# The merge gates beside a triangular solve: eight wide pieces against seven narrow Strassen pieces

## What is computed

```python
rq, rk, rv, rg, gqkv, gz, ga, gb, mg_ret, mg_gdn = jnp.split(u @ w_in, SPLIT_IDX, axis=-1)
...
a_mat = jnp.einsum("bhnid,bhnjd->bhnij", kb, kc) * jnp.where(strict, decay_incl, 0.0)
lhs = jnp.eye(CHUNK) + a_mat
u = lax.linalg.triangular_solve(lhs, vc * bc, left_side=True, lower=True, unit_diagonal=True)
...
merged = jax.nn.sigmoid(mg_ret) * y_ret + jax.nn.sigmoid(mg_gdn) * y_gdn
return h + merged @ w_out
```

## Time and profile before

| what | value |
|---|---|
| median of three runs | 2882.27 us |
| the profiled execution, its own time | 2882.01 us |
| its span, first to last instruction | 2880.2 us |
| TensorE busy | 2747.2 us (95%) |
| DVE, ACT, POOL busy | 1401.9, 483.1, 164.8 us |
| chain that ended last | TensorE 83%, issue 10%, DVE 4% |
| mean granted TensorE clock | 0.973 |

### The profile page before, as it was taken

How to read it: one execution, slowest core, us unless ns; L and a number is a source line. 1 busy time by engine, 2 the same in 40 slices (tenths; PEclk the granted TensorE clock), 3 DMA queues, 4 the chain that set the end, 5 groups by cost and what they waited for, 6 DMA issues and landing times.

```text
span 2880.2 us, 41833 instructions
## 1 busy us (share of the span) xinstructions
PE 2747.2 (95%) x18538; PEld 2415.2 (84%) x18538; DVE 1401.9 (49%) x1876; ACT 483.1 (17%) x775; POOL 164.8 (6%) x155
## 2 busy tenths in 40 slices
PE   8999899999999989999999999899889989997998
PEld 5778788999687878899998877686789988876998
DVE  5573223895657232533331000156559766776454
ACT  1261110101136111110000000023121022112110
POOL 0002210000000321000000000000000001010000
PEclk9999999999999999999999999999789989998999
DMA  7341214885434212345445888735158634441442
GB/s 264 127 158 67 74 59 165 324 317 185 146 132 161 74 59 74 106 161 175 158 166 169 290 286 288 239 117 176 57 200 337 263 119 162 139 151 62 161 161 89
DMA packets 211924, 476.40 MB, mean 165 GB/s; under 512 B 7584, under 2 KB 36896, under 8 KB 211488
## 3 DMA queue, kind: packets, MB, share of 16 engines
q1 hardware_dynamic: 211168, 472.26, 47.0%
q10 hardware_dynamic: 576, 1.46, 0.1%
HBM read 472.64 MB, written 1.05 MB: 164 GB/s over the span
## 4 chain that ended last, share of the span: by engine, by line
PE 83%; issue 10%; DVE 4%; ACT 1%; DMA 1%; POOL 1%; SPq 0%; POOLq 0%; DVEq 0%; ACTq 0%
PE ps L462 17%; PE ps L1720 17%; PE ps L530 11%; PE ps L522 8%; PE ps L2229 7%; PE ps L1961 4%; PE ps L1915 4%; PE ps L2258 3%; PE ps L1168 1%; PE ps L1179 1%; PE ps L1175 1%; PE ps L2268 1%; PE ps L737 0%; PE ps L1041 0%; PE ps L2201 0%
## 5 line engine op out<-in xcount | busy, mean ns | idle before, releaser
L462 PE MATMUL ps<-uT,ring 128*128 128x256 f32 x1280 | 292.7, 384 | 18.6 <-DMA ring<-in_w_in 9.4
L462 PEld LDWEIGHTS ps<-uT,ring 128*128 128x128 f32 x1280 | 242.5, 193 | 51.3 <-issue 9.3
L2229 PEld LDWEIGHTS ps<-work,ring 128*128 128x128 f32 x1760 | 198.6, 192 | 5.1 <-issue 4.8
L2229 PE MATMUL ps<-work,ring 128*128 128x128 f32 (+4 forms) x1760 | 198.4, 275 | 0.0
L1720 PE MATMUL ps<-uT,ring 128*128 128x128 f32 x1584 | 192.0, 281 | 3.2 <-ACT uT L895 2.5
L1720 PEld LDWEIGHTS ps<-uT,ring 128*128 128x128 f32 x1584 | 188.1, 198 | 5.5 <-issue 5.2
L462 PE MATMUL ps<-xn,ring 128*128 128x256 f32 x768 | 174.2, 385 | 9.6 <-issue 6.9
L1720 PE MATMUL ps<-xn,work 128*128 128x128 f32 x1584 | 179.8, 275 | 0.0
L1720 PEld LDWEIGHTS ps<-xn,work 128*128 128x128 f32 x1584 | 178.3, 192 | 0.0
L462 PEld LDWEIGHTS ps<-xn,ring 128*128 128x128 f32 x768 | 146.7, 194 | 30.9 <-issue 11.3
L530 PEld LDWEIGHTS ps<-uT,ring 128*128 128x128 f32 x1152 | 135.4, 197 | 5.9 <-issue 5.8
(11 more groups left out here) (458 smaller groups left out, 4496.7 us busy)
## 6 DMA issues: line engine op xcount, KB each, us to landing
ring<-in_w_in SPq DMA_DIRECT2D x72, 1024.0 KB, 5.1
work<-in_ada_w SPq DMA_DIRECT2D x48, 1024.0 KB, 10.8
ring<-in_exp_w_down SPq DMA_DIRECT2D x40, 1024.0 KB, 5.1
ring<-in_attn_w_in SPq DMA_DIRECT2D x36, 1024.0 KB, 5.1
ring<-in_exp_w_gate SPq DMA_DIRECT2D x32, 1024.0 KB, 5.6
ring<-in_exp_w_up SPq DMA_DIRECT2D x32, 1024.0 KB, 6.4
ring<-in_ffn_w_in SPq DMA_DIRECT2D x32, 1024.0 KB, 7.4
ring<-in_ffn_w_out SPq DMA_DIRECT2D x22, 1024.0 KB, 8.4
```

What stands on the lines that cost most here:

```text
L462: mm = pe.matmul(acc[:, m * T:(m + 1) * T], w[:, k, m * P:(m + 1) * P], src[:, half * 4 + k, :], start=(half == 0 and k == 0 and m % 2 == ...
L2229: mm = pe.matmul(acc[:, m * c:(m + 1) * c], w[:, k, m * P:(m + 1) * P], picked[:, half * 4 + k, OFFS[i]:OFFS[i] + c], start=(half == 0 and ...
```

## The change

The four gate units of a layer are computed by Strassen's scheme on a half layer each: the unit's 1024 x 512 weights as 2 x 2 blocks of 512 x 256, the input as 2 x 2 blocks of 512 rows by 128 tokens. A unit then takes seven phases of eight products (128 x 128 weights, 128 tokens) in place of eight pieces of four. A half has 22 steps in place of 24. New on DVE: four sums of token blocks per layer (128 x 512), four weight sums per unit (128 x 1024, in place in the ring), four adds of output blocks per unit (128 x 256). New on ACT: four snaps per unit (128 x 256). The sigmoid works in place in SBUF after the last add. Both slabs of a unit are freed at P7. One PSUM bank holds two products' blocks, so P2 waits for the snap of P1, and P5 for that of P4.

```diff
-        BESIDE = (("mgret", 0), ("brret", 0), ("mgret", 1), ("brret", 1), ("mggdn", 0), ("mggdn", 1))
+        gate_tq = [area(4 + 0.5 * i, 512).rearrange("p (k t) -> p k t", t=P) for i in range(4)]
+        GATE_PHASES = ("P1", "P4", "P2", "P5", "P6", "P3", "P7")
+        def gate_phase_pe(pe, l, name, j, what):
...
+            if what == "P1":
+                slab_wait(pe, gate_slab[unit])
+                w, x_, to, start = A["A11"], B11, acc["a"], True
+            elif what == "P4":
+                slab_wait(pe, gate_slab[unit] + 1)
+                pe.wait_ge(gate_tq_ready, l + 1)
+                w, x_, to, start = A["A22"], T4, acc["d"], True
+            elif what == "P2":
+                pe.wait_ge(q_snap, 4 * Q + 1)
+                w, x_, to, start = A["A12"], B21, acc["b"], False
+            elif what == "P5":
+                pe.wait_ge(q_sum, 4 * Q + 1)
+                pe.wait_ge(q_snap, 4 * Q + 2)
+                w, x_, to, start = A["A22"], T1, acc["c"], False
+            elif what == "P6":
+                pe.wait_ge(q_sum, 4 * Q + 3)
+                pe.wait_ge(q_out, 4 * Q + 1)
+                w, x_, to, start = A["A11"], T2, acc["a"], False
+            elif what == "P3":
+                pe.wait_ge(q_sum, 4 * Q + 4)
+                pe.wait_ge(q_snap, 4 * Q + 3)
+                w, x_, to, start = A["A12"], B22, acc["c"], False
+            else:
+                pe.wait_ge(q_snap, 4 * Q + 4)
+                w, x_, to, start = A["A21"], T3, acc["a"], False
+            for m in range(2):
+                for k in range(4):
+                    mm = pe.matmul(to[:, m * P:(m + 1) * P], w[:, k, m * P:(m + 1) * P], x_[:, k, :],
+                                   start=(start and m == 0 and k == 0), stop=True, skip_group_check=True)
...
+            if half == 0:
+                return iter(gate("mgret", 0) + branch(0) + gate("mgret", 1))
+            return iter(branch(1) + gate("mggdn", 0) + gate("mggdn", 1))
...
-                for i in range(2):
-                    beside_pe(pe, l, 24 * half + 2 * (n - h0) + i)
-            for i in range(8, 12):
-                beside_pe(pe, l, 24 * half + i)
+                for i in range(2 if n + 1 < h0 + HALF else 1):
+                    next(beside)(pe)
+            for i in range(3):
+                next(beside)(pe)
...
+            act.wait_ge(q_out, 4 * quad_no[unit] + 4)
+            gate = sg[2 * (br == "gdn") + j]
+            act.activation(gate, gate, ACT.Sigmoid).then_inc(tick(sig_out), 1)
...
+                if half == 0 and n == 0:
+                    (B11, B12), (B21, B22) = token_blocks(uT)
+                    T1, T2, T3, T4 = gate_tq
+                    dstep(dve, dve.tensor_tensor(T1, B12, B11, ALU.subtract))
+                    dstep(dve, dve.tensor_tensor(T2, B22, T1, ALU.subtract))
+                    dve.tensor_tensor(T4, T2, B21, ALU.subtract)
+                    dve.tensor_tensor(T3, B22, B12, ALU.subtract).then_inc(tick(gate_tq_ready), 1)
...
+                if half == 0 and n < 3:
+                    gate_sums_dve(dve, early, *((0, 1), (2,), (3,))[n])
+                if half == 0 and n == 1:
+                    gate_add_dve(dve, early, early_sg, "11")
+            if half == 0:
+                gate_add_dve(dve, early, early_sg, "12", "21", "22")
...
+            if half == 1:
+                gate_sums_dve(dve, early, 0, 1, 2)
...
+                if lev == 3:
+                    if half == 0:
+                        merge_dve(dve, l, "ret", 0)
+                    else:
+                        gate_add_dve(dve, early, early_sg, "21", "22")
...
-                if half == 0 and lev == 2:
-                    merge_dve(dve, l, "ret", 0)
+                if half == 1 and lev == 1:
+                    gate_add_dve(dve, early, early_sg, "11")
+                    gate_sums_dve(dve, early, 3)
+                if half == 1 and lev == 2:
+                    gate_add_dve(dve, early, early_sg, "12")
+                if lev == 4:
+                    gate_sums_dve(dve, late, 0, 1, 2)
+                    if half == 0:
+                        dve.wait_ge(merged_out, 4 * l + 1)
+                    gate_add_dve(dve, late, late_sg, "11")
+                if lev == 5:
+                    gate_sums_dve(dve, late, 3)
+                if lev == 6:
+                    gate_add_dve(dve, late, late_sg, "12", "21", "22")
```

More of the change, by code:

```diff
@@ new lines, in gate_wait, with gate_snap_act @@
+        def gate_wait(eng, unit, what):
+            if what == "P7":
+                eng.wait_ge(slab_used, gate_slab[unit] + 2)
+            else:
+                eng.wait_ge(q_phase, Q_PHASES * quad_no[unit] + GATE_PHASES.index(what) + 1)
+        def gate_snap_act(act, unit, *which):
+            acc = gate_sums(unit)
+            where = {"P1": "a", "P4": "d", "P5": "c", "P6": "a"}
+            for what in which:
+                if what == "P1":
+                    act.wait_ge(q_out, 4 * quad_no[unit])
+                gate_wait(act, unit, what)
+                act.activation(gate_snap[what], acc[where[what]], ACT.Copy).then_inc(tick(q_snap), 1)
@@ new lines, in gate_sums_dve @@
+        def gate_sums_dve(dve, unit, *parts):
+            Q, A = quad_no[unit], gate_weights(unit)
+            for part in parts:
+                if part == 0:
+                    gate_wait(dve, unit, "P4")
+                    out_, a, b, op = "A22", "A21", "A22", ALU.add
+                elif part == 1:
+                    dve.wait_ge(q_sum, 4 * Q + 1)
+                    out_, a, b, op = "A21", "A11", "A21", ALU.subtract
+                elif part == 2:
+                    gate_wait(dve, unit, "P1")
+                    dve.wait_ge(q_sum, 4 * Q + 2)
+                    out_, a, b, op = "A11", "A22", "A11", ALU.subtract
+                else:
+                    gate_wait(dve, unit, "P2")
+                    dve.wait_ge(q_sum, 4 * Q + 3)
+                    out_, a, b, op = "A12", "A12", "A11", ALU.subtract
+                dve.tensor_tensor(A[out_], A[a], A[b], op).then_inc(tick(q_sum), 1)
@@ new lines, in gate_add_dve @@
+        def gate_add_dve(dve, unit, dst, *which):
+            Q, acc = quad_no[unit], gate_sums(unit)
+            f = lambda x: x.rearrange("p (m t) -> p m t", t=P)
+            d4 = dst.rearrange("p (m t) -> p m t", t=T)
+            for what in which:
+                i, t = int(what[0]) - 1, int(what[1]) - 1
+                out_ = d4[:, 2 * i:2 * i + 2, t * P:(t + 1) * P]
+                if what == "11":
+                    gate_wait(dve, unit, "P2")
+                    dve.wait_ge(q_snap, 4 * Q + 1)
+                    i_ = dve.tensor_tensor(out_, f(gate_snap["P1"]), f(acc["b"]), ALU.add)
+                elif what == "12":
+                    gate_wait(dve, unit, "P3")
+                    dve.wait_ge(q_snap, 4 * Q + 4)
+                    i_ = dve.tensor_tensor(out_, f(gate_snap["P6"]), f(acc["c"]), ALU.add)
+                elif what == "21":
+                    gate_wait(dve, unit, "P7")
+                    i_ = dve.tensor_tensor(out_, f(acc["a"]), f(gate_snap["P4"]), ALU.subtract)
+                else:
+                    i_ = dve.tensor_tensor(out_, f(gate_snap["P5"]), f(acc["a"]), ALU.add)
+                i_.then_inc(tick(q_out), 1)
+            if "22" in which:
+                free(unit)
@@ L1107, in beside_pe, with beside_steps, branch_pe @@
+        def beside_steps(l, half):
+            gate = lambda name, j: [lambda pe, what=what: gate_phase_pe(pe, l, name, j, what) for what in GATE_PHASES]
+            branch = lambda j: [lambda pe, i=i: branch_pe(pe, l, j, i) for i in range(8)]
+            if half == 0:
+                return iter(gate("mgret", 0) + branch(0) + gate("mgret", 1))
+            return iter(branch(1) + gate("mggdn", 0) + gate("mggdn", 1))
+        def branch_pe(pe, l, j, i):
+            name = "brret"
             part, m = i // 4 % 2, i % 4
@@ L1146, in solve_pe @@
             h0 = half * HALF
+            beside = beside_steps(l, half)
             spread(h0)
@@ L1169, in solve_pe @@
                 mm.then_inc(tick(psum_full), 1)
-                beside_pe(pe, l, 24 * half + 10 + 2 * lev)
+                next(beside)(pe)
                 pe.wait_ge(m_out, 6 * s + lev)
@@ L1180, in solve_pe @@
                 mm.then_inc(tick(psum_full), 1)
-                beside_pe(pe, l, 24 * half + 11 + 2 * lev)
+                next(beside)(pe)
             pe.wait_ge(x_out, 13 * s + 13)
@@ L1545, in decay @@
                 free(unit)
+            early = f"mgret{l}0" if half == 0 else f"mggdn{l}0"
+            late = f"mgret{l}1" if half == 0 else f"mggdn{l}1"
+            early_sg, late_sg = (sg[2 * half + j] for j in range(2))
             decay(h0)
```

58 lines of the change are left out of this document (45 added, 13 removed).

## The result

| | kernel before | with the change |
|---|---|---|
| median of six runs each, same chip | 2879.85 us (2877.52 to 2883.3) | 2891.47 us (2889.2 to 2894.72) |
| profiled execution, its own time | 2882.01 | 2893.02 |
| its span | 2880.2 | 2891.2 |
| TensorE, DVE, ACT, POOL busy | 2747.2, 1401.9, 483.1, 164.8 | 2750.7, 1458.9, 495.6, 173.4 |
| mean granted clock | 0.973 | 0.967 |

The ratio is 1.004, with an interval of 1.003 to 1.005: slower by 11.6 us where 2.1 was forecast, and above the range. 56 narrow phases took the place of 64 wide pieces, by the prediction's count 10.8 us less TensorE work at full clock, and yet TensorE is busy 3.5 us longer.

The account below looks back on a forecast made before the run. TensorE was taken to bound the solve, its chain having no gap. Fewer pieces, less added waits, restarts and tail delays, gave +2.1 us on 2882.01, so 2884.1 us; range 2876 to 2890, bounds 2877.8 to 2888.9.

Parts of the forecast that it names:

- The pieces and narrow phases: Gate units: eight wide pieces take 13.84 us, seven narrow phases 12.5; 10.8 less for eight units if nothing waits.
- the sum: Whole kernel: first halves lose 2.16 and 2.76 us, second halves win 1.4 each, in all +2.1 us.
- P4 waited: Half 0, head 0: TensorE waits for token sums taking turns with POOL, 2.4 us in layer 0, 3.0 in layer 1.
- P3 waited: Half 0, head 2: TensorE waits 0.65 us for the fourth sum in DVE's long queue; bounds 0 and 1.5.
- the piece after P7: Half 0: the next unit waits 0.85 us for a slot DVE frees, 1.1 with restart; 0.47 won against before.
- level 3: Late unit's P1 waits for its slot: 0.66 us in half 0, 0.17 in half 1; 0.9 and 0.4 with restart.
- The other sums: Level 4 in both halves, and before p1 in half 1: the sums fit into DVE's rests and cost nothing.
- the clock falls at P4: Rival: the wait at P4 lowers TensorE's clock; a fall in both layers adds 5.6 us, 2889.7; chance 0.15.
- Its aside on the tail's waits: Tail of each half: three waits of 1.6, 0.8 and 0.7 us might lower the clock, 2.8 us each.
- Its main condition: At P4: the clock falls from a wait of some 3 us on; waits of 2.4 and 3.0 were forecast.
- The rule on narrow passes: Skill's figures would make a narrow phase 1.30 us against 0.78, some 26 us over 56 phases; the prediction rejected this.
- Layer 0's share: Layer 0's solve entered the total in full: first half loses 2.16 us, second half wins 1.4.

Follow-up runs that it names:

- the wait alone: Kernel before, plus four unused token sums on DVE at head 0 of half 0, the second wide piece waiting for them: 2889.78 us, ratio 1.0033.
- the token sums early: The change with three token sums moved ahead of the first decay and the fourth behind head 0's masking: 2883.82 us, median of twelve runs.
- all edits together: The change with token sums moved early, U1's copy before the sigmoid, two pieces in the pause, head 4's decay inside the head norm: 2864.65 us, ratio 0.9948.

## Why the prediction was wrong

**The pieces and narrow phases** were right: x0 of layer 0's first half at -0.01 us from its old time (0.0 by the sum), and half 1 shorter by 3.34 from its second head's spread to x0, in both layers (3.35).

**The waits** were right too, as idle times of TensorE with the forecast in brackets. The token sums took turns with POOL and ended at 225.57 (225.8); P4 waited 2.28 (2.4), in layer 1 2.33 (3.0). P3 waited 0.46 (0.65), the piece after P7 1.05 (0.85, so 0.30 was won there and not 0.47), level 3 0.66 and 0.19 (0.66 and 0.17). The other sums brought no wait. In layer 0 the first half's r came 2.15 late (2.16). No term of waits or work was off by more than 0.7 us.

**The step that failed is "the sum"**. It put nothing for the clock, which it left to a rival, and nothing, without a reason, for what stands behind the solve. Of the 8.9 us between its +2.1 and the profile's +11.0, 4.9 lie inside the solve (some 5.5 of TensorE at half clock, less 0.6 of waits that were shorter than forecast; of the 5.5, layer 1's P4 and first tail are 4.5 and layer 0's gram stage after the pause, at 0.89 in place of 0.91, some 0.7) and 5.2 behind it, at a lower clock too; 1.6 were won back between the layers, and 0.4 stand at the start and the end. The weight of the rival "the clock falls at P4" was too low with it: 0.15, at 2889.7. That rival was nearly the result, but its mechanism only in part, so its number is half luck. Its place was half right: P4 of layer 1 lost 1.6, P4 of layer 0 nothing. Its aside on the tail's waits was the larger part: 2.9 us beyond the wait itself in layer 1, in both profiles, and in the second 2.9 in layer 0 as well. Its main condition, a wait of some 3 us, was not met: P4's 2.33 in layer 1 went with a fall, and so did waits of 1.52, 0.78 and 0.69 one after another, though a wait of 1.3 had cost nothing in the earlier trace rows. To measure the longest single wait against the 3.82 of the pause was the wrong use of the earlier trace rows.

**What no rival had** is the loss behind the solve: 5.2 us from 1123 to 2029, in both profiles of the change and in neither of the kernel before. The prediction summed the solve and took the rest as fixed. The narrow phases are not needed for this loss: the kernel before with the pause filled has 5.1 of it, and with U1's copy first and the decay moved as well 4.8. With the wait alone none of it appeared, but 4 us were lost at a transfer 1300 us later. It is shown that the time there is TensorE at a lower granted clock with the same work and the same idle time, and that it differs between executions of one kernel. What sets it is not shown: neither the amount added nor the end of the solve orders the runs, and the groups of times inside one kernel stay unexplained. For this half of the loss the cause is open.

**The rule on narrow passes** was rightly refused: with the change 16 passes take 1.79 or 1.80 in the chain, where no wait stands before them. By the Trainium skill's figures (TensorE: Matmul & The Clock Gate, Back-to-back issue gap) they would have taken the half us more that the prediction estimated; the trace after disagrees as the one before did.

**Layer 0's share** was counted fully; in both profiles of the change its 1.45 and 4.2 are reduced by 1.6 before layer 1 begins, 0.9 of it a wait for a transfer that a second profile of the kernel before shows at 0.2.

## What to carry to other kernels

Price an added wait of TensorE at its length, and let the range reach to twice that: here two waits of 2.3 us, alone, cost 9.8 where their length is 4.6. Before work is taken from a full TensorE, look for where it stands still anyway and put the work that is left there: the same seven phases that lost 11.6 us belong to a version that wins 15.4 once the token sums use DVE's rest, the copy that the next product needs goes before the sigmoid that nobody waits for, and the pause between the halves is filled. Most of the win is not the seven phases: without them, with U1's copy first, the pause filled and the decay moved, it is 11.9. And take two profiles of a kernel whose runs fall into groups before reading a difference of under 5 us.

## What was not expected of the hardware

Two-operand sums of DVE and POOL's masks slow each other both ways: DVE's 0.69 became 0.85 to 1.48, POOL's 1.00 up to 1.45 (layer 1). With POOL idle the sums took 0.69 again, and the one left beside its masks took 1.02. Executions of one kernel on one chip fell into groups 5 to 14 us apart (2873 and 2888 for the token sums early); in the two profiles of that kernel the granted clock of a few stretches accounts for nearly all of the 15.2 us. Three short waits close together, 1.52, 0.78 and 0.69 us, can go with a fall of the clock (10 tails of 24) where 0.69, 0.78 and 0.69 never did (0 of 52, with the 0.71 of the kernel before counted in). A version with less work or fewer waits before a stretch can have a lower clock in it: all edits together were 23.0 us ahead at 1123 and 16.9 at 2029, with a granted clock of 0.80 in the stretch from 1193 to 1237 where the kernel before has 0.88.
